# A two-layer encoder with routed experts: gate and up of the next expert moved ahead of this expert's down products

## What is computed

```python
def run_block(args):
    xb, e = args
    return (jax.nn.silu(xb @ w_gate[e]) * (xb @ w_up[e])) @ w_down[e]
...
y = yb.reshape(rows, d) * row_w[:, None].astype(xf.dtype)
return jax.ops.segment_sum(y, row_tok, num_segments=t)
```

## Time and profile before

| | us |
|---|---|
| median of 3 runs | 1660.23 |
| lowest and highest of these | 1658.36, 1663.84 |
| the profiled execution | 1657.52 |
| its span, first to last instruction | 1655.7 |
| TensorE busy | 1375.0 |
| DVE busy | 383.6 |
| ScalarE busy | 341.3 |
| GpSimd busy | 217.9 |
| moved by DMA | 472.65 MB |

### The profile page before, as it was taken

One profiled execution on the slowest core, in us unless ns is written; L12 is line 12 of the kernel. 1 busy time (PEld: TensorE's weight loads), 2 busy tenths in 40 slices (PEclk: granted clock), 3 DMA queues, 4 the chain that ended last, 5 costly groups with the idle time before them and its releaser, 6 DMA issues. The chain is left out here.

```text
span 1655.7 us, 17674 instructions
## 1 busy us (share of the span) xinstructions
PE 1375.0 (83%) x6689; PEld 768.3 (46%) x6689; DVE 383.6 (23%) x721; ACT 341.3 (21%) x657; POOL 217.9 (13%) x380
## 2 busy tenths in 40 slices
PE   5999994999888787786999878895999878788882
PEld 5999772333232232234667655774333223223230
DVE  3434423000000000005522476623000000000003
ACT  5223320100000000004534354421010000000002
POOL 2000000122111111101000132101111111111111
PEclk9999996999999999997999989996999999999996
DMA  9120427999999999985121200316999999999994
GB/s 342 40 103 1 166 95 325 415 425 426 425 426 426 426 425 426 425 346 210 51 96 58 102 1 1 141 50 274 402 425 425 425 427 426 425 424 423 425 381 163
DMA packets 60921, 472.65 MB, mean 285 GB/s; under 512 B 10592, under 2 KB 10668, under 8 KB 35776
## 3 DMA queue, kind: packets, MB, share of 16 engines
q1 hardware_dynamic: 46480, 441.48, 64.4%
q0 software_dynamic: 14384, 30.36, 4.9%
HBM read 465.17 MB, written 23.13 MB: 295 GB/s over the span
## 5 line engine op out<-in xcount | busy, mean ns | idle before, releaser
L958 PE MATMUL ps<-ring,act 128*64 128x512 f32 x1792 | 442.1, 646 | 76.1 <-DMA ring<-in_e_up 70.3
L958 PEld LDWEIGHTS ps<-ring,act 128*64 128x64 f32 x1792 | 139.6, 142 | 373.9 <-issue 373.9
L925 PE MATMUL ps<-parts 128*128 128x512 f32 (+1 forms) x1104 | 266.5, 400 | 7.2 <-DVE parts L1226 6.6
L981 PE MATMUL ps<-ring,act 128*64 128x512 f32 x896 | 204.6, 597 | 31.0 <-ACT act L773 31.0
L1409 DVE TENSOR_TENSOR act<-act,ps 128x256 f32<-128x256 f32 x64 | 27.0, 421 | 868.8 <-ACT act L771 868.8
L925 PEld LDWEIGHTS ps<-parts 128*128 128x128 f32 (+1 forms) x1104 | 195.1, 179 | 68.5 <-DVE parts L1226 4.6
L911 PE MATMUL ps<-parts 128*128 128x264 f32 x1152 | 144.9, 288 | 4.5 <-DVE parts L1221 2.9
L911 PEld LDWEIGHTS ps<-parts 128*128 128x128 f32 x1152 | 143.5, 191 | 5.5 <-issue 5.5
L771 ACT ACTIVATE act<-ps 128x256 f32<-128x256 f32 x64 | 24.6, 384 | 572.0 <-PE ps L958 572.0
L981 PEld LDWEIGHTS ps<-ring,act 128*64 128x64 f32 x896 | 70.8, 136 | 126.2 <-issue 126.2
L1221 DVE TENSOR_TENSOR parts<-ring,parts 128x1024 fp32r<-128x1024 f32 x64 | 77.8, 1225 | 118.8 <-ACT parts L704 118.7
(11 more groups left out here) (164 smaller groups left out, 921.4 us busy)
## 6 DMA issues: line engine op xcount, KB each, us to landing
ring<-in_e_gate SPq DMA_DIRECT2D x56, 2048.0 KB, 18.2
ring<-in_e_up SPq DMA_DIRECT2D x56, 2048.0 KB, 22.5
ring<-in_e_down SPq DMA_DIRECT2D x56, 2048.0 KB, 22.4
arena<-in_e_down SPq DMA_DIRECT2D x8, 2048.0 KB, 15.7
ring<-in_a_w_in SPq DMA_DIRECT2D x6, 2048.0 KB, 19.7
arena<-in_e_up SPq DMA_DIRECT2D x6, 2048.0 KB, 19.2
arena<-in_e_gate SPq DMA_DIRECT2D x6, 2048.0 KB, 14.2
ring<-in_w_kv SPq DMA_DIRECT2D x4, 2048.0 KB, 13.6
```

The lines of the kernel that those rows point to most:

```text
L925: last = mm(bank, x[:, k, :], w[:, k, :], start=(k == 0 and i == 0), stop=(k == KC - 1 and i == 2))
L958: last = mm(ps[f * C:(f + 1) * C, 2 + b, :].rearrange("p (g m i) -> p g m i", g=2, i=2), x, w, start=(k == 0), stop=(k == KC - 1))
L981: last = mm(ps[o * C:(o + 1) * C, 6 + b, :], hT[:, b, (2 * c + a) * C:(2 * c + a + 1) * C], w[:, f * D + o * DH:f * D + (o + 1) * DH], sta ...
```

## The change

TensorE's order becomes: gate and up of expert n+1, transpose of the block of n+2, transpose of the hidden block of n, down of n. At a layer's start gate and up of expert 0 come first; then the block of expert 1 is transposed and its gate and up follow. The last expert of a layer has no expert behind it: TensorE ends with hidden transpose and down of 30, gate and up of 31, hidden transpose and down of 31. GpSimd gathers the rows of n+3 ahead of the scatter of n. DVE copies out the block of n+2 behind the product of expert n. The counters of freed buffers are renamed: one counts `gate_up`, one `down`, and SP and ScalarE wait on these. The order and the number of SP's loads, the buffers and the arithmetic stay.

```diff
 # SP
-                sp.wait_ge(unit_used, free_at[n % RING] if wait is None else wait)
+                if uses is None:
+                    sp.wait_ge(*free_at[n % RING])
+                else:
+                    sp.wait_ge(done[part], uses)
...
-                    load(q * 2 + u, u, part, q * 6 + (U_MOE[layer] + 3 * (u - len(LEAD) - 2) + done[part]))
+                    load(q * 2 + u, u, part, q * 2 + (E * layer + u - 1))
 # GpSimd
-                            pool.wait_ge(x_turned, E * layer + q * 2 + u + 1)
-                            gather(u, q * 2 + u + 2, n)
+                        pool.wait_ge(x_turned, q * 2 + (E * layer + u + 2))
+                        gather(1 - u, q * 2 + u + 3, q * 4 + 3 + 2 * u)
+                        pool.wait_ge(y_ready, q * 2 + (E * layer + u + 1))
+                        scatter(u, q * 2 + u, q * 4 + 4 + 2 * u, None if first else q * 16)
 # ScalarE
-                        if lead:
-                            act.wait_ge(lead_used, lead_done(layer, 2 * q + u) + 1)
-                        else:
-                            act.wait_ge(unit_used, ring_uses(layer, q, u, early) + 2)
+                        act.wait_ge(gate_up_done, q * 2 + (E * layer + u + 1))
 # TensorE
+                def products(q, u, early):
...
+                    pe.wait_ge(xT_ready, q * 2 + (E * layer + u + 1))
+                    gate_up(u, w, lead_half_used if early and q == u == 0 else None).then_inc(gate_up_done, 1)
+
+                def finish(q, u, early):
+                    pe.wait_ge(hidden_ready, q * 2 + (E * layer + u + 1))
+                    turn_hidden(u).then_inc(hidden_turned, 1)
...
+                    pe.wait_ge(hT_ready, q * 2 + (E * layer + u + 1))
+                    down(u, w).then_inc(down_done, 1)
+
+                def pair(q, early):
                     for u in range(2):
+                        if u == 0:
+                            products(q, 1, early)
+                        else:
+                            products(q + 1, 0, early and q + 1 < EARLY)
+                        pe.wait_ge(gathered[layer][u], q * 16 + 32)
+                        turn_block(u).then_inc(x_turned, 1)
+                        finish(q, u, early)
...
+                finish(PAIRS - 1, 0, False)
+                products(PAIRS - 1, 1, False)
+                finish(PAIRS - 1, 1, False)
 # DVE
-                        if not (last and u == 1):
-                            dve.wait_ge(x_turned, E * layer + q * 2 + u + 2)
-                            take_x(1 - u).then_inc(xT_ready, 1)
+                        if not last:
+                            dve.wait_ge(x_turned, q * 2 + (E * layer + u + 3))
+                            take_x(u).then_inc(xT_ready, 1)
```

More of the change, by code:

```diff
@@ L52 @@
 UNIT = KC * W
+IN_RING = [e for e in range(E) if e not in LEAD]
 U_IN, U_AOUT = 0, 6
@@ L447, in experts, with load @@
             def experts(layer):
-                done = {"gate": 2, "up": 2, "down": 3}
-                def load(ex, u, part, wait):
+                done = {"gate": gate_up_done, "up": gate_up_done, "down": down_done}
+                def load(ex, u, part, uses):
                     n = U_MOE[layer] + 3 * u + ORDER.index(part)
-                    sp.wait_ge(unit_used, free_at[n % RING] if wait is None else wait)
+                    if uses is None:
+                        sp.wait_ge(*free_at[n % RING])
+                    else:
+                        sp.wait_ge(done[part], uses)
                     expert_load(layer, part, bass.ds(ex, 1), ring[:, n % RING, :], ring_landed[n % RING])
-                    free_at[n % RING] = U_MOE[layer] + 3 * (E - len(LEAD) - 2 + u) + done[part]
+                    free_at[n % RING] = done[part], E * layer + E - 1 + u
                 def load_lead(ex):
-                    i = LEAD.index(ex)
-                    if i == 1:
+                    uses = E * layer + LEAD[LEAD.index(ex) - 1] + 1
+                    if ex == LEAD[1]:
                         for a in range(2):
@@ L500, in experts @@
                         for part in ORDER:
-                            load(ex, ring_turn(ex) % 2, part, U_MOE[layer] + 3 * (ring_turn(ex) - 2) + done[part])
+                            load(ex, ring_turn(ex) % 2, part, E * layer + IN_RING[ring_turn(ex) - 2] + 1)
                 with sp.Fori(EARLY, PAIRS) as q:
@@ L607, in moe @@
-                with pool.Fori(1, PAIRS - 1) as q:
-                    pair(q, False, False)
-                pair(PAIRS - 1, False, True)
+                pool.wait_ge(x_turned, E * layer + 1)
+                gather(0, 2, 2)
+                pair(0, True)
+                with pool.Fori(1, PAIRS - 2) as q:
+                    pair(q, False)
+                pool.wait_ge(x_turned, E * layer + E - 2)
+                gather(1, E - 1, 2 * E - 5)
+                for ex in range(E - 4, E):
+                    pool.wait_ge(y_ready, E * layer + ex + 1)
+                    scatter(ex % 2, ex, 2 * E - 4 + ex - (E - 4), 16 * (ex // 2))
@@ L780, in pair @@
                         nc.scalar.copy(y_out[:, u, :], ps[:, 6 + u, :]).then_inc(y_ready, 1)
-                for q in range(EARLY):
-                    pair(q, True)
-                with act.Fori(EARLY, PAIRS) as q:
+                pair(0, True)
+                with act.Fori(1, PAIRS) as q:
                     pair(q, False)
@@ L1025, in moe @@
                 table_rows(0, nt).then_inc(tabled, 1)
-                def pair(q, early, last_pair):
-                    for u in range(2):
[L1029 to L1034, removed]
-                        else:
[L1036 to L1056, removed]
@@ L1058, in moe @@
-                pe.wait_ge(gathered[layer][0], 16)
-                turn_block(0).then_inc(x_turned, 1)
+                def products(q, u, early):
+                    if early and 2 * q + u in LEAD:
+                        pe.wait_ge(lead_landed, lead_landing(layer, 2 * q + u))
+                        w = lead_w
+                    else:
+                        (gs, gv), (us, uv) = (expert_unit(layer, q, u, part, early) for part in ("gate", "up"))
+                        pe.wait_ge(ring_landed[gs], gv)
+                        pe.wait_ge(ring_landed[us], uv)
+                        w = ring[:, gs:us + 1, :]
+                    pe.wait_ge(xT_ready, q * 2 + (E * layer + u + 1))
+                    gate_up(u, w, lead_half_used if early and q == u == 0 else None).then_inc(gate_up_done, 1)
@@ new lines, in finish @@
+                def finish(q, u, early):
+                    pe.wait_ge(hidden_ready, q * 2 + (E * layer + u + 1))
+                    turn_hidden(u).then_inc(hidden_turned, 1)
+                    if early and 2 * q + u in LEAD:
+                        pe.wait_ge(lead_down_landed, 16 * (len(LEAD) * layer + LEAD.index(2 * q + u) + 1))
+                        w = lead_down
+                    else:
+                        ds, dv = expert_unit(layer, q, u, "down", early)
+                        pe.wait_ge(ring_landed[ds], dv)
+                        w = ring[:, ds, :]
+                    if not (early and q == 0):
+                        pe.wait_ge(y_ready, q * 2 + (E * layer + u - 1))
+                    pe.wait_ge(hT_ready, q * 2 + (E * layer + u + 1))
+                    down(u, w).then_inc(down_done, 1)
```

69 lines of the change are left out of this document (31 added, 38 removed).

## The result

The changed kernel takes 1718.5 us (median of 4 runs, 1718.2 to 1725.3) against 1660.2 us before: a ratio of 1.0362, 95% interval 1.0339 to 1.0385. It is slower by 58 us. The forecast was 1706 us, slower, in a range of 1670 to 1738 us.

The account below looks back on a forecast made before the run. The weights' stream was taken to set the pace. Head 6.3, middle 14.8 and end 3.0 us make 24.1 us a layer, 48.2 us for two, on 1657.5 us: 1706 us, range 1670 to 1738 us.

Parts of the forecast that it names:

- rival C: TensorE's chain decides: 0.35 us saved in each of 64 chains, -22 us, 1635 us; chance 0.03.
- (1) The head: Start of a layer: the load of down of expert 3 goes out 8.7 us later; 6.3 us a layer.
- (2) The middle: Experts 12 to 31, loads two deep: late down loads cost 0.78 us an expert, 14.8 us a layer.
- the alternation: Middle: warm and slow experts take turns, starts of gate and up 15.6 and 17.1 us apart.
- the chain after idling: Middle: from start of gate and up to release of the down load, 14.3 us after idling, 12.8 us warm.
- the sum's own line: Middle: two periods are the chain, 0.2 us to start, 2.6 us extra for a load and 15.56 us for three matrices.
- a load's extra cost: Middle: a load costs more than its share of the stream, taken as 2.6 us.
- a warm expert: Middle: an expert not slowed by idling, load out at 12.83 us, costs next to nothing.
- (3) The end: End of a layer: down of 30 now precedes gate and up of 31; 3.0 us a layer.
- Rival A: Middle: the queue doesn't run dry, only head and end cost; 19 us, 1676 us; chance 0.18.
- rival B: Middle: the queue runs dry for every expert, all run slow, 1.9 us more a period; 1748 us; chance 0.12.

Follow-up runs that it names:

- experiment 4: The kernel before with GpSimd's part alone (gather of n+3 ahead of the scatter of n), all else as it was: 1659.7 us, ratio 0.9989.
- experiment 1: The changed kernel with SP issuing loads in the order of use, gate and up of n+1 ahead of down of n: 1671.7 us, ratio 1.0061.
- experiment 5: The changed kernel with the first expert's down put back ahead of gate and up of expert 1 in each layer: 1712.5 us, ratio 1.0320.
- experiment 9: The kernel before with one later wait: from expert 11 on, SP loads down of n+2 only when down of n+1 is done: 1719.3 us, ratio 1.0357.
- experiment 2: The changed kernel with four unread matmuls after each down in the loop over pairs 5 to 14: 1711.8 us, ratio 1.0314.
- experiment 8: The changed kernel with four unread matmuls (2 us) ahead of the transpose of the hidden block instead of behind down: 1739.1 us, ratio 1.0481.

## Why the prediction was right, and where its sizes were off

**What bounds the kernel** was read rightly: taking the wait out of each expert's chain brought nothing in the total, and rival C (TensorE's chain decides) did not occur. It did shorten the period where TensorE sets it, at the start of a layer, and by 0.58 us instead of 0.35. The early gather cost nothing, as said (experiment 4), and with the loads in the order of use the mean period is 15.66 and 15.58 us, so the reordered copies cost nothing in the middle either (experiment 1).

**(1) The head**, 6.3 us: 5.8 and 7.5 us measured. The load went out 23.6 us after the start, 9.1 us later than before, for 8.7 predicted. What the sum had not seen is that the same holds for down of 4 (experiment 5).

**(2) The middle**, 14.8 us: 22.2 and 16.5 us. The mechanism is the predicted one, down to the alternation, only wider (15.0 and 18.0 us above, for 15.6 and 17.1): experiment 1 takes it away without touching TensorE, experiment 9 makes it without the change. The mis-sized term is the chain after idling, taken as 14.3 us from one gate and up of 8.87 us. With 4 us idle and more, which the sum's own periods gave (17.1 less 12.8), gate and up take up to 10.3 us; where they take 9.8, the sum's own line (5.4 + 9.8 + 0.2 + 2.6 + 15.56) gives 33.6 us for two periods, and 318.4 us over 19 periods are 33.5. That an expert always slows after 2 us idle was read too simply from the earlier trace rows: expert 19 of the kernel before took 7.42 us after 2.25.

The 2.6 us for a load's extra cost held. It can be read off load by load: take the time from the issue of a down load to the landing of the up matrix two loads behind it, less 15.56 us. In the middle of the changed kernel and of experiments 2, 8 and 9, 59 down loads went out less than 1.6 us before the up matrix ahead of them landed, or after it; for these the median is 2.7 us (2.2 to 3.4, one of 4.1).

The statement that a warm expert costs next to nothing did not hold: in experiment 2 gate and up take 7.8 and 8.0 us in the mean of experts 11 to 30 of the two layers, and the period stays 0.7 and 0.9 us too long. By the sum's line that is an extra cost of 3.7 to 3.8 us (2 x 16.33 - 5.4 - 7.8 - 0.2 - 15.56), but this isn't the price of a dry queue: most of these loads went out while the matrix ahead was still 2.4 to 5.5 us from landing. The stream loses time even so. Over the same four kernels, the distance from one up matrix landing to the next was longer than 15.56 us in all 18 cases where a down load went out 2.4 to 3.4 us before that landing, by 0.3 to 2.7 us, and by 0.3 us at most, or not at all, in all 32 where it went out 4.5 us or more before. In experiment 2, for instance, the down load at 667.84 us goes out 3.25 us before the up matrix at 671.09 lands, and the next up matrix lands 17.92 us later. Between 3.4 and 4.5 us it was mixed (33 cases, up to 1.2 us longer, half of them not longer at all). So in these runs the stream stayed full for certain only if the load came more than 4 us before the queue was empty. The sum's warm expert is one of the other cases: its load goes out 12.83 us after a start, and the matrix ahead lands 15.4 us after it (15.56 less 0.2), so only 2.5 us later.

The Trainium skill (DMA: Bandwidth & Descriptors, Anatomy of one DMA) has about 2.0 us as the fixed cost of one DMA, for the path through GpSimd. The loads here are issued by SP, and their 2.7 us are above that; so the choice of 2.6 us from the rows was the better one.

**(3) The end**, 3.0 us: 5.8 and 7.1 us. The steps were right one by one (1.7 us of copies and silu, 4.7 us to the end of down). I had let expert 30 run warm; it ran slow (9.69 us), so in layer 0 down of 30 ended 20.8 us after its start and not 19.2. In layer 1 its down was slow as well (5.35 us for 3.65). Another 0.8 us is a matter of counting: the last of the sum's 19 starts is that of expert 31, which the table has in the end.

**The sum:** 24.1 us a layer were forecast, 33.8 and 31.1 measured in the profiled execution. The head was about right and the other terms too low, so no large error made up for another. Rival A (the queue doesn't run dry) is refuted by the 9.3 us to landing, rival B by the alternation: only about every second expert is slow.

**Why 27 us and not 38 in experiment 8:** the expectation took the price of a load as the same in both kernels. In experiment 8, 17 of 37 down loads went out less than 1.6 us before the matrix ahead landed or after it, in experiment 2 only 10 of 38. So part of the longer chain only used up queue that was left. This fits the loads read one by one; no run tests it alone.

**Open:** why a stream that still has 2.4 to 3.4 us of work queued loses up to 2.7 us, and why the loss differs so much from case to case. The views read here don't separate the 16 DMA engines, and no run was made for it.

## What to carry to other kernels

When a change reorders the consumer of a stream of loads, ask when each buffer comes free and in which order the loads are issued, before counting what the consumer saves. In a queue that waits in order, one buffer released late holds every load behind it; the time from issue to landing tells how much queue is left (22 us here before, 9 us after), more plainly than the share of busy DMA (1.00 and 0.95 from 440 to 740 us). A load that goes out only 2.4 to 3.4 us before the queue is empty came too late here. If the consumer's order changes, change the order of the loads with it: that alone gave back 47 of 58 us.

## What the hardware did that I had not expected

The price of idling isn't one number: in the kernel before, after 2.1 to 2.8 us idle, gate and up took either 7.4 us or 8.8 to 9.0 us; in the changed one, after 2.1 to 6.2 us idle, between 8.7 and 10.3 us, and not always more after a longer gap (8.77 us after 5.88, 9.69 after 4.21). And holding the clock at 0.98 instead of 0.90 by padding gave only 7 of 58 us: on this stretch, bound by loads, the slow clock follows from the waits more than it causes them.
